# Causal mask on the diagonal block: set by GpSimd on the gates, in place of a bf16 matmul on the scores

## The reference, cut to what matters

```python
z = jnp.einsum('bqhd,bkhd->bhqk', qi, k) * scale
mask = key_pos[None, :] < t[:, None]                  # strictly causal
log_1m_beta = jnp.where(mask, jax.nn.log_sigmoid(-z), 0.0)
rev = lax.cumsum(log_1m_beta, axis=3, reverse=True)
excl = jnp.concatenate([rev[..., 1:], jnp.zeros_like(rev[..., :1])], axis=-1)
w = jnp.where(mask, jnp.exp(log_beta + excl), 0.0)
out = jnp.einsum('bhqk,bkhd->bqhd', w, v)
```

## Time and profile before

| | before |
|---|---|
| median of 3 runs | 1233.47 us (1233.45 to 1234.15) |
| the profiled execution's own time | 1233.28 us |
| its span, first to last instruction | 1231.4 us |
| granted TensorE clock, mean | 0.995 |
| TensorE busy | 97% |
| VectorE busy | 55% |
| GpSimd busy | 39% |
| bf16 mask matmuls | 64 |

### The profile page before, as it was taken

The page is one execution under the profiler, slowest core; times in us unless marked ns, Lnnn a source line. Parts: engine busy times, 40 slices in busy tenths (PEclk is TensorE's granted clock), DMA queues, the critical chain, the costliest instruction groups (busy, mean ns, idle before and its releaser), DMA issues.

```text
span 1231.4 us, 15527 instructions
## 1 busy us (share of the span) xinstructions
PE 1191.3 (97%) x6108; PEld 999.3 (81%) x6108; DVE 680.0 (55%) x733; ACT 422.1 (34%) x785; POOL 478.5 (39%) x363
## 2 busy tenths in 40 slices
PE   6999999999999999989999999999999999999996
PEld 5899889889888878877787888887878788878875
DVE  5349994985966855576334344443434343434346
ACT  5311451441453834553414141414131313132322
POOL 4112301301300002245828292929282828283721
PEclk9999999999999999999999999999999999999998
DMA  7203202202105211113121211121212121112113
GB/s 269 77 18 88 69 18 59 69 12 70 35 1 172 95 35 35 38 33 102 35 69 35 69 35 69 35 69 35 69 35 69 35 69 35 69 35 69 35 52 137
DMA packets 65334, 75.50 MB, mean 61 GB/s; under 512 B 6064, under 2 KB 54828, under 8 KB 65262
## 3 DMA queue, kind: packets, MB, share of 16 engines
q1 hardware_dynamic: 64078, 72.38, 18.9%
q10 hardware_dynamic: 1184, 2.13, 0.5%
HBM read 63.92 MB, written 6.32 MB: 57 GB/s over the span
## 4 chain that ended last, share of the span: by engine, by line
PE 74%; POOL 12%; issue 7%; ACT 2%; DVE 2%; DMA 1%; POOLq 0%; SPq 0%; ACTq 0%; DVEq 0%
PE ps L1656 18%; PE ps L1635 17%; PE ps L1463 15%; PE ps L1524 7%; PE ps L1584 5%; POOL wa_lo L586 4%; PE ps L1424 4%; PE ps L1493 3%; PE ps L1511 3%; POOL wb_lo L586 2%; POOL wa_f L607 1%; POOL wa_f L601 1%; POOL wa_f L604 1%; DMA out<-ost 1%; POOL wb_f L601 1%
## 5 line engine op out<-in xcount | busy, mean ns | idle before, releaser
L1344 DVE TENSOR_TENSOR mix<-ps,mix 128x512 f32<-128x512 f32 x176 | 121.3, 691 | 137.6 <-PE ps L1656 137.6
L1106 DVE SCALAR_TENSOR_TENSOR acc<-u_pad,par,acc 128x1024 f32<-128x1024 f32 x116 | 146.6, 1303 | 0.3
L540 POOL TENSOR_TENSOR wp_lo<-raw,wp_hi 128x1024 fp32r<-128x1024 f32 x16 | 60.7, 3796 | 213.6 <-ACT wp_hi L685 213.6
L1656 PE MATMUL ps<-wd_hi,act_hi 128*128 128x512 f32 x352 | 137.1, 389 | 1.4 <-DVE act_lo L1333 1.4
L1656 PE MATMUL ps<-wd_hi,act_lo 128*128 128x512 f32 x352 | 136.9, 389 | 0.0
L1656 PE MATMUL ps<-wd_lo,act_hi 128*128 128x512 f32 x352 | 136.9, 389 | 0.0
L586 POOL TENSOR_TENSOR wa_lo<-wa_f,wa_hi 128x512 fp32r<-128x512 f32 x58 | 79.4, 1372 | 133.0 <-ACT wa_hi L907 129.1
L1463 PE MATMUL ps<-hn_hi,wp_hi 128*128 128x348 f32 (+2 forms) x352 | 118.5, 337 | 0.0
L1463 PE MATMUL ps<-hn_lo,wp_hi 128*128 128x348 f32 (+2 forms) x352 | 117.6, 334 | 0.0
L1463 PE MATMUL ps<-hn_hi,wp_lo 128*128 128x348 f32 (+2 forms) x352 | 117.5, 334 | 0.0
L1635 PE MATMUL ps<-t_hi,wa_hi 128*128 128x512 f32 x232 | 91.9, 396 | 4.3 <-POOL wa_lo L586 3.9
(11 more groups left out here) (160 smaller groups left out, 2584.4 us busy)
## 6 DMA issues: line engine op xcount, KB each, us to landing
raw<-in_w_gate SPq DMA_DIRECT2D x11, 1024.0 KB, 5.3
raw<-in_w_up SPq DMA_DIRECT2D x11, 1024.0 KB, 5.3
wd_f<-in_w_down SPq DMA_DIRECT2D x11, 1024.0 KB, 4.9
raw<-in_w_in SPq DMA_DIRECT2D x16, 512.0 KB, 3.8
xin<-in_x SPq DMA_DIRECT2D x8, 512.0 KB, 10.8
wo_raw<-in_w_out SPq DMA_DIRECT2D x4, 1024.0 KB, 8.2
mix<-in_x SPq DMA_DIRECT2D x8, 512.0 KB, 3.5
out<-ost SPq DMA_DIRECT2D x8, 512.0 KB, 2.6
```

The source lines that it names most:

```text
L540: pool.tensor_tensor(dst, raw[:, slot, :], hi.bitcast(F32), ALU.subtract).then_inc(wlo_done, 1)
L1106: dve.scalar_tensor_tensor(out=acc[:, j % 2, :], in0=u, scalar=w, in1=acc[:, j % 2, :], op0=ALU.mult, op1=ALU.add).then_inc(conv_step, 1)
L1344: dve.tensor_tensor(hrow, ps[:, TB + n % 4, :], hrow, ALU.add).then_inc(d_added, 1)
L1656: last = pe.matmul(ps[:, TB + n % 4, :], a[s][:, t, i * P:(i + 1) * P], w_[m][:, t, dh * BANK:(dh + 1) * BANK], start=(t == 0 and s == m = ...
```

## The change

The bf16 identity and mask and the 64 mask matmuls go; the second score matmul of each chunk closes the accumulation. GpSimd gets one instruction for each unit: on the 128x128 diagonal block of `gq` it keeps the gates below the diagonal and writes 1.0 elsewhere (`mask(p, n)`). It waits for ScalarE's last sigmoid of the unit (`z_free`) and raises a new semaphore `z_masked`, for which the scan waits in place of `z_free`. In GpSimd's order the masks stand between the low parts of the weights: three low parts, masks 0 to 6, one low part, masks 7 to 15, in pairs 0 to 2; masks alone in pair 3. Two memsets and two selections go from GpSimd's start.

```diff
@@ gpsimd
-            pool.memset(ident_bf[:, :], 0.0).then_inc(consts, 1)
-            pool.memset(mask_bf[:, :], -1e30).then_inc(consts, 1)
...
-            for kind, p in WEIGHTS[4:]:
-                lo_weight(kind, p)
+            def mask(p, n):
+
+                d0 = FRONT + META + UNITS[n][1] * P
+                pool.wait_ge(z_free, past(NZ * p + CZ[n + 1]))
+                pool.affine_select(out=gq[:, n % BUFS, d0:d0 + P], in_=gq[:, n % BUFS, d0:d0 + P], compare_op=ALU.is_ge,
+                                   fill=1.0, base=-1, pattern=[[-1, P]], channel_multiplier=1).then_inc(z_masked, 1)
+
+            for p in range(PAIRS):
+                for kind, q in WEIGHTS[4 + 4 * p:7 + 4 * p]:
+                    lo_weight(kind, q)
+                for n in range(NU):
+                    mask(p, n)
+                    if n == 6:
+                        for kind, q in WEIGHTS[7 + 4 * p:8 + 4 * p]:
+                            lo_weight(kind, q)
@@ vector
-                    dve.wait_ge(z_free, past(NZ * p + CZ[n + 1]))
+                    dve.wait_ge(z_masked, NU * p + n + 1)
@@ tensor
                         for part in range(2):
                             last = pe.matmul(ps[:, Z_BANKS[m], 0:cols], qst[:, h, i * P:(i + 1) * P],
                                              kd[:, h, part, c0:c0 + cols], start=(part == 0),
-                                             stop=(part == 1 and c0 + used <= d0))
-                        lo, hi = max(d0, c0), c0 + used
-                        if hi > lo:
-                            last = pe.matmul(ps[:, Z_BANKS[m], lo - c0:hi - c0], ident_bf[:, :],
-                                             mask_bf[:, lo - d0:hi - d0], start=False, stop=True)
+                                             stop=(part == 1))
                         last.then_inc(z_ready, 1)
```

More of the change, by code:

```diff
@@ L178, in hybrid_block @@
         ident = keep("ident", [P, P], F32)
-        ident_bf = keep("ident_bf", [P, P], BF16)
-        mask_bf = keep("mask_bf", [P, P], BF16)
         par = keep("par", [P, 4, NP], F32)
@@ L229, in hybrid_block @@
         u_zeroed, conv_step = sem("u_zeroed"), sem("conv_step")
-        z_ready, z_free, scanned = sem("z_ready"), sem("z_free"), sem("scanned")
+        z_ready, z_free, z_masked, scanned = sem("z_ready"), sem("z_free"), sem("z_masked"), sem("scanned")
         front_zeroed, t_ready, t_copied, pv_used, pv_evac = sem("front_zeroed"), sem("t_ready"), sem("t_copied"), sem("pv_used"), sem("pv_evac")
@@ L515, in _ @@
             pool.memset(zeros[:, :], 0.0).then_inc(consts, 1)
-            pool.wait_ge(consts, 6)
+            pool.wait_ge(consts, 4)
             pool.affine_select(out=ident[:, :], in_=ident[:, :], compare_op=ALU.not_equal, fill=1.0,
                                base=0, pattern=[[-1, P]], channel_multiplier=1).then_inc(consts, 1)
[L519 to L523, removed]
             def root(src, v, dst, scale, ready, n, v_sem, r_sem):
@@ L1028, in _ @@
             dve.sem_inc(conv_step, 1)
-            dve.wait_ge(consts, 6)
+            dve.wait_ge(consts, 4)
             def norm_x(t):
@@ L1397, in _ @@
                 pe.sem_inc(s, 1)
-            pe.wait_ge(consts, 9)
+            pe.wait_ge(consts, 5)
             def transpose_x(t):
@@ L1484, in scores @@
                         pe.wait_ge(*freed("q", i // 4, p))
-                    d0 = META + i * P
-                    for c, (c0, cols, used) in enumerate(z_chunks(i)):
+                    for c, (c0, cols, _) in enumerate(z_chunks(i)):
                         m = CZ[n] + c
```

## The result

| | before | changed |
|---|---|---|
| median | 1233.81 us (6 runs, 1233.14 to 1234.8) | 1243.47 us (6 runs, 1243.17 to 1245.68) |
| ratio | | 1.0082, 95% interval 1.007 to 1.0094 |
| the profiled execution's own time | 1233.28 us | 1243.54 us |
| its span | 1231.4 us | 1241.5 us |
| granted TensorE clock, mean | 0.995 | 0.989 |

The change makes the kernel 0.8% slower. The time lies in the range, 1.5 us above the forecast of 1242.0.

What follows compares the result with a forecast made beforehand. TensorE and its few waits, as ahead of scores 4, were taken to bound the kernel. Late scans net of matmuls 5.6, pair 3 -0.5, clock 3.6: 8.7 us on 1233.28 gives 1242.0 us, range 1237.5 to 1246.5 (8 in 10).

Steps and rivals of the forecast that it cites:

- What bounds the kernel: TensorE, busy 97% of the span, and its few waits: 0.76 us ahead of scores 4 in each pair, behind VectorE.
- The matmuls: Removing TensorE's mask matmuls frees 0.07 us each for units 4 to 15: 0.84 us a pair, 3.4 us in four.
- The late scan in pairs 0 to 2: Mask 0 behind GpSimd's third low part makes scores 4 2.7 us late; net 1.9 us a pair, 5.6 in three.
- The first reading of the 7.15 us: GpSimd's third low part waits 4.75 us for VectorE, then works 2.40; all 2.40 remain when VectorE stops.
- a slow pace beside the taps: Other reading: the low part runs slowly beside VectorE, with 0.7 us of its 2.40 done when VectorE stops.
- The fourth low part: Between masks 6 and 7, it costs scan 7 2.1 us as before, nothing more; VectorE is 8.4 us ahead.
- Pair 3: No low part there; scan 0 and scores 4 0.35 us late, net -0.5 us (-0.8 to +1.5).
- The clock: TensorE's idle time drops its clock in each of pairs 0 to 2: 1.2 us each, 3.6 in all.
- No fall of the clock: Rival: TensorE's clock does not fall in the pairs, or only once: 1238.4 us, to 1239.8; chance 0.27.
- Masks get in each other's way at every unit: Rival: GpSimd's masks and VectorE collide throughout, 1 to 5 us more a pair, 1245 to 1255 us; chance 0.1.
- Faster: Rival: low part finds an earlier gap, scan 0 under 1 us late; 1228.8 us if nothing waits; chance 0.07.
- It nets out: Rival: scan 0's delay only 2.0 us, pair 3 gives 0.8, clock holds: 1235.4 us or less; chance 0.07.

Runs made afterwards that it cites:

- e2: Kernel before without its 64 mask matmuls and nothing in their place (causal mask of the diagonal block left out): 1228.3 us, ratio 0.9955.
- e5: Changed kernel with 14 throw-away matmuls in each of pairs 0 to 2, where TensorE idles: 1239.43 us, ratio 1.0046 to the kernel before.
- e1: Changed kernel with GpSimd's masks 0 and 1 ahead of the third low part in pairs 0 to 2: 1242.62 us, ratio 1.007 to the kernel before.
- e6: Changed kernel, pairs 0 to 2: masks 0 and 1 first, third low part waits until scan 1 is done: 1230.37 us, ratio 0.9973 to kernel before.
- e7: Kernel before, mask still a matmul, but scan 0 waits for the third low part in pairs 0 to 2: 1243.59 us, ratio 1.0084.
- e9: Changed kernel with units 0 and 1 of every pair masked by matmul, the other 14 by GpSimd: 1230.18 us, ratio 0.9971 to the kernel before.
- e10: Changed kernel with both late low parts (third and fourth) behind mask 15: 1229.31 us, ratio 0.9968 to the kernel before.
- e11: Changed kernel with the edits of e9 and e10 together: 1230.28 us, ratio 0.9974 to the kernel before.
- e3: Changed kernel with the bf16 mask matmuls kept as well as GpSimd's selections: 1248.15 us, ratio 1.0122 to the kernel before.

## Why the prediction was right

**What bounds the kernel.** Right: scores 4 of each pair follow the low part of q, and what delayed scan 0 arrived there undiminished, 2.6 us at the scan and 2.7 at scores 4 in pair 1.

**The matmuls.** Mis-sized: 0.84 us a pair by 0.07 for each of 12, 3.4 in all; e2 measured 1.0 a pair, 4.1 in the attention. Two things were left out. The masks of units 0 and 1 stand ahead of the last projection group, which makes q, so they did count a little: in pair 1 it is 8.73 us from scores 0 to scores 4 before and 8.66 in e2, and VectorE's idle time ahead of the low part of q went from 0.10 to 0.03 us. And the 0.07 us is the interval to the next matmul's start; where a projection group or scores follow a mask directly, more goes with it (the 24 matmuls of that group take 5.64 us up to scores 2 before, 5.54 in e2).

**The late scan in pairs 0 to 2.** Right in size, 2.7 us, and net: 1.9 us a pair forecast, 1.8, 1.8 and 1.7 in e5. The first reading of the 7.15 us was the right one: nothing of the low part is done beside the taps. The Trainium skill ("SBUF — State Buffer", section "Who interferes with whom") says that a VectorE instruction with two SBUF inputs contends with a GpSimd instruction that reads SBUF, and that the lock is exclusive. The trace of the changed kernel agrees: the low part ends at 235.55, 2.3 us after the second tap does (233.27), so practically all of its 2.40 us was still to be done; a slow pace beside the taps would have left 1.7. That the place ahead of mask 0 is what matters was only half of it: e1 has the masks ahead and nearly the same delay. What matters is whether a low part is already waiting when VectorE stops ahead of the low part of q. In e6 VectorE stops too, for 0.19 us, but the low part is held back, and its pairs 1 and 2 are only 0.4 and 0.3 us longer than those of e2; in e7 there is no mask to wait for, but the low part is let in, and the whole delay is back.

**The fourth low part** and the masks of later units cost nothing on the chain, as said: in the changed kernel and in e5 VectorE idles 2.44 us ahead of scan 7 in each of pairs 0 to 2, and yet the pairs of e5 are only 1.8 us longer than before, which the late scan 0 accounts for.

**Pair 3.** Right: 0.19 us of idling ahead of scan 0, pair 0.6 us shorter (forecast 0.5).

**The clock.** Right that it falls in each of the three pairs, mis-sized: 3.6 us forecast, 6.3 by e5, since two of the three stretches were 6.8 us long, which the prediction had named as its upper case. The argument by the length of the idle time alone was too simple: e7 with nearly the same delay had one fall in its profiled execution, and e6 had one behind 1.6 us of idle time in two pieces.

**The sum.** The net of late scan and matmuls in pairs 0 to 2 was 5.6 us forecast and is 5.3 by e5; pair 3 was -0.5 and is -0.6; the clock was 3.6 and is 6.3. These make 11.0 us where 8.7 were forecast. Outside the pairs 0.9 us was gained, for which the prediction has no term and which no run explains; that leaves 10.1 us between the two spans. That the total came within 1.5 us is in part luck: 0.9 us without a cause stood against a clock term that was 2.7 us too small.

**The rivals.** "No fall of the clock" would have been 1239.4 (e5). "Masks get in each other's way at every unit" is out by e6. "Faster" took 4.5 us for what the matmuls are worth, near the 4.1 of e2, and is what e6, e9, e10 and e11 reach once the low part is out of the way. "It nets out" is out: the delay was 2.6 us at the scan and not 2.0, and the clock fell.

## What to carry to other kernels

Work moved to GpSimd can be paid in VectorE's time, as here, where VectorE's taps and scans have two inputs in SBUF and GpSimd's low parts read SBUF too. Look where the instructions that GpSimd already has find their gap, and whether the new wait opens an earlier one in a worse place. An order by hand is then worth more than the move itself; here the same 64 selections cost 9.7 us (the changed kernel) or give 3.7 to 4.8 (e6, e10), by the place of one or two instructions of 2.4 us. Leaving two masks of sixteen where they were was as good (e9). Idle time of TensorE, 3.0 us in pair 1, cost more than its length here, so price the clock with it.

## What the runs showed of the hardware

- 64 selections of 128x128 took 789 ns in the mean in the changed kernel, the shortest 282 and the longest 2945, and 294 in the row of a selection that ran alone. Two took 0.53 us together while VectorE waited (235.50). I take the difference for waiting on VectorE; no run tests this by itself. The group of them:

```profile
L561 POOL TENSOR_SCALAR_AFFINE_SELECT gq<-gq 128x128 f32<-128x128 f32 x64 | 50.1, 789 | 111.6 <-ACT gq L813 111.4
```

- VectorE passed from one instruction with two SBUF inputs to the next four times without letting the waiting low part in (229.0, 230.2, 230.8 and 232.0 in the earlier trace rows); in e1, behind a short idle time of VectorE, it got in at such a change (234.45). What decides whose turn it is stays open.
- A fall of the clock cost 1.4 us with a stretch of 3.4 us and 2.2 to 2.7 us with one of 6.8 (e5 against the changed kernel). In the profiled executions it fell in three pairs of three with scan 0 late by 2.55 us (the changed kernel, e3), in one of three with 2.37 us (e7), and in one of three with 0.19 us (e6, where e10 with the same had none). Throw-away matmuls in the idle time prevented it (e5).
